# First part routed head by head, first tile's group norm in halves, output projection begun from the heads, one hold of the gathers taken out

## The chip, the core and the metric

The kernel runs on one core of one Trainium2 chip. The metric is the device time in microseconds (us) of one execution; less is better. The engines that matter here are TensorE (PE; its weight loads are PEld), VectorE (DVE), ScalarE (ACT), GpSimd (POOL), which issues the expert gathers, and SyncE (SP), which issues the weight and input transfers. Each engine works through its own instructions in the order written, and semaphores tie the engines together.

## What is computed

One layer of a decoder for a prompt of 512 tokens and a sample group of 8 x 4 tokens, model width 1024, all in float32. Cut to what matters here:

```python
p = rmsnorm(x) @ w_in                      # q, k, v, o for 4 heads; gates; a and g for the convolution
h = mlstm_chunkwise(q, k, v, gates, state) * sigmoid(o)
u = a * sigmoid(g)
c = silu(group_norm(depthwise_conv(u, 31 taps)))   # 8 groups of 64 channels
x = x + concat([h, c]) @ w_out
xn = rmsnorm(x)
q = xn @ w_query                           # 8 heads, two halves of 128
s1, s2 = q_half1 @ keys1, q_half2 @ keys2
# per token and head: top 16 of s1, top 16 of s2, top 16 of their sums -> 16 expert numbers
act = gelu(einsum(xn, u_tab[experts]))     # 128 rows of 1024 floats per token
x = x + einsum(softmax(scores) * act, v_tab[experts])
y = rmsnorm(x)
```

Each token reads 128 rows of the u table and 128 of the v table, 4 KB each.

## The kernel before, in words

**Tiles and groups.** The tokens make five tiles: tiles 1 to 4 are 128 prompt tokens each, tile 0 is the 32 sample tokens. The mixer works in three groups, (1), (2 and 0), (3 and 4). The experts are worked in the order 1, 2, 0, 3, 4. A pick is one expert number per partition: 128 picks for a prompt tile, 32 for the sample tile (its tokens are spread over four quadrants), 544 in all. Pick n needs one u gather and one v gather, 128 rows or 0.524 MB each. 32 picks (two of the eight heads) are a part; there are 17 parts, and part 9 (picks 288 to 319) is the first of tile 3.

**Gathers.** POOL issues them in the order of PLAN (`plan_gathers`, line 67): the u gathers run LEAD = 44 picks ahead of the v gathers, then u and v alternate. At a pick in LATE_PICKS, which are the first picks of tile 2 (128) and tile 3 (288), no u gather is issued before all v gathers below it. Every gather needs a free slot of 4 KB per partition: 12 slots at first, 14 from pick 160, 30 from pick 352 on (JOIN_AT), where weights and mixer buffers are no longer needed. A u gather also waits until its part's expert numbers exist (`picked`), a v gather for their transposed copy. A u slot comes free when VectorE has done its dot product (`dot_product`, line 1039), a v slot when TensorE has added a group of four (`experts`, line 859) into the PSUM tile y. The y tile is shared, so a tile's first group waits for the `final` of the tile before.

**Routing.** VectorE finds a part's expert numbers: `top_lists` (the best 16 of four score columns, two per head), `candidates` (sums of pairs and their best 16) and `experts_of` (a search by comparison over 16 x 50, per head). Between these steps it can take dot products (`between`).

**Order.** The mixer's steps are written out by hand for each engine; after each step an engine calls `keep`, which takes gather work up to a number that a list sets for that step: DOTS_BY (dot products on VectorE), QUADS_BY (groups of four v's on TensorE), GATES_BY (ACT). ROUTE_AT and ROUTE_DOTS say after which step and at which dot a part is routed, GATE_AT when its z columns are made, FINAL_AT when a tile's last norm is done. Two PSUM banks take all products of the mixer in turn (`order_of_banks`); a job needs the job two before it evacuated.

**First tile.** TensorE projects w_in in 24 weight tiles of 0.5 MB from a ring of four slots; SP requests the next one when the job that used the slot is done. VectorE does the 31 taps of the convolution for the channel chunks 0, 1 and then 2, 3 (`convolutions`). After it the four chunks are centred, squared, averaged, rooted, scaled and passed through silu together (`by_group`, `centre`, `squares`, `deviations`, `scale`, `silus`; NORMS names which chunks go together). Only then the output projection runs, eight jobs of 128 columns (`output`, `residual`), then transposes, queries and scores. `routing(1, 0)` starts when the four score columns of two heads are there; the first gather waits for it.

## Time and profile before

| | us |
|---|---|
| median of 3 runs | 1776.27 |
| range | 1767.8 to 1779.16 |
| profiled execution | 1774.04 |
| its span | 1772.2 |
| busy: PE / DVE / ACT / POOL | 1064.4 / 1065.0 / 333.7 / 1056.1 |

The profile is of one execution; its span goes from the first to the last instruction. Busy time is the sum over the span of one engine's instructions; the engines overlap. Of the expert work, VectorE has 462 dot products into slots of the ring (430 of them with the prompt's x, 1218 ns each), TensorE the v products (L884). The chain of waits that ended last splits the span into PE 27%, DMA 25%, DVE 20%, POOL 16%, issue 7%, ACT 3%. In the page's strip of forty slices the transfer rate is 206, 164 and 266 GB/s in the first three and about 409 in most of those after the middle; the lowest later ones are 309, 336, 321 and 264.

### The profile page before, as it was taken

The numbers are of one execution on the slowest core, as the hardware profiler recorded it, in microseconds if no ns is written. First come the engines' busy times: TensorE is split into PE (matmuls) and PEld (weight loads), VectorE is DVE, ScalarE is ACT, GpSimd is POOL, SyncE is SP. The second block draws the span as 40 slices with busy tenths as digits, with TensorE's granted clock in tenths as the row PEclk, the third lists the DMA queues.
The fourth block names the chain that finished last, engine by engine and source line by source line (L and its number), as shares of the span: only waits on it lengthen the run. The fifth ranks groups of instructions, "written<-read, shape, count | busy, mean of one in ns | idle before, by whom it ended". The sixth has DMA issues, their size and how long they took to land.

```text
span 1772.2 us, 18241 instructions
## 1 busy us (share of the span) xinstructions
PE 1064.4 (60%) x6249; PEld 657.5 (37%) x6249; DVE 1065.0 (60%) x2715; ACT 333.7 (19%) x874; POOL 1056.1 (60%) x1131
## 2 busy tenths in 40 slices
PE   7898457978796938887894477023333433333344
PEld 6787446756674726666662011000000000000000
DVE  5547796665693198575464703995757585845420
ACT  3232113653141213540221000000000000000000
POOL 2005356666453576675556755747777777777771
PEclk9899789979898978998997588555555666566668
DMA  6589999999998999998999999969999999999997
GB/s 206 164 266 397 359 399 391 353 351 410 412 367 309 403 406 409 408 409 336 409 410 409 362 347 321 410 264 409 409 410 409 410 409 411 409 409 410 409 409 290
DMA packets 192850, 659.75 MB, mean 372 GB/s; under 512 B 32336, under 2 KB 32344, under 8 KB 192632
## 3 DMA queue, kind: packets, MB, share of 16 engines
q0 software_dynamic: 156672, 570.49, 82.1%
q1 hardware_dynamic: 35512, 86.01, 13.7%
q10 hardware_dynamic: 576, 2.10, 0.3%
q8 instruction: 51, 0.84, 0.2%
q14 instruction: 39, 0.32, 0.0%
HBM read 652.96 MB, written 5.16 MB: 371 GB/s over the span
## 4 chain that ended last, share of the span: by engine, by line
PE 27%; DMA 25%; DVE 20%; POOL 16%; issue 7%; ACT 3%; SPq 2%; ACTq 0%; POOLq 0%; DVEq 0%
DMA ring<-in_u_experts,expert_idx 14%; DVE ring L1053 10%; POOL ring L594 9%; PE y L884 9%; DMA ring<-in_v_experts,expert_idx_by_token 9%; PE pp L635 8%; PE pp L645 4%; PE pp L711 3%; POOL C_sample L594 2%; SPq L483 2%; DMA act_T<-in_v_experts,expert_idx_by_token 1%; POOL w_ring L594 1%; DVE hit L1410 1%; DVE lists L1412 1%; DVE hit L1408 1%
## 5 line engine op out<-in xcount | busy, mean ns | idle before, releaser
L1053 DVE SCALAR_TENSOR_TENSOR ring<-ring,x_normed 128x1024 f32<-128x1024 f32 x430 | 514.4, 1218 | 335.2 <-DMA ring<-in_u_experts,expert_idx 332.7
L594 POOL DMA_INDIRECT ring<-in_u_experts,expert_idx x462 | 446.1, 966 | 409.6 <-DVE expert_idx L1417 118.7
L884 PE MATMUL y<-ring,z_columns 128*32 128x512 f32 x1364 | 398.9, 761 | 228.5 <-DMA ring<-in_v_experts,expert_idx_by_token 114.0
L594 POOL DMA_INDIRECT ring<-in_v_experts,expert_idx_by_token x313 | 302.3, 966 | 161.1 <-issue 76.6
L635 PE MATMUL pp<-act_T,w_ring 128*128 128x128 f32 (+2 forms) x1728 | 299.1, 333 | 87.5 <-DVE scratch L1232 31.9
L635 PEld LDWEIGHTS pp<-act_T,w_ring 128*128 128x128 f32 x1728 | 266.3, 200 | 127.1 <-issue 88.7
L884 PE MATMUL y<-C_sample,z_columns 128*32 128x512 f32 x316 | 199.8, 907 | 85.2 <-DMA ring<-in_v_experts,expert_idx_by_token 72.0
L884 PE MATMUL y<-w_ring,z_columns 128*32 128x512 f32 x180 | 139.3, 1002 | 182.5 <-DMA ring<-in_v_experts,expert_idx_by_token 161.7
L884 PEld LDWEIGHTS y<-ring,z_columns 128*32 128x32 f32 x1364 | 77.7, 127 | 374.6 <-issue 299.3
L645 PE MATMUL pp<-w_ring,act_T 128*128 128x128 f32 (+1 forms) x960 | 122.1, 289 | 39.8 <-DVE scratch L1247 14.1
L645 PEld LDWEIGHTS pp<-w_ring,act_T 128*128 128x128 f32 (+1 forms) x960 | 115.6, 187 | 53.8 <-issue 38.8
L884 PEld LDWEIGHTS y<-w_ring,z_columns 128*32 128x32 f32 x180 | 21.5, 153 | 270.6 <-issue 270.6
L711 PE MATMUL pp<-u_prompt,tap_diag 128*128 128x128 f32 (+1 forms) x496 | 91.5, 344 | 3.6 <-ACT tap_diag L1671 3.6
L1775 ACT ACTIVATE score_minus_max<-score_minus_max 128x16 f32<-128x16 f32 x34 | 7.0, 206 | 456.3 <-DVE ring L1053 425.3
L1671 ACT ACTIVATE tap_diag<-ident,w_dw 128x128 f32<-128x128 f32 x248 | 84.7, 394 | 34.9 <-PE pp L711 32.3
L711 PEld LDWEIGHTS pp<-u_prompt,tap_diag 128*128 128x128 f32 x496 | 80.6, 197 | 20.7 <-issue 13.4
L594 POOL DMA_INDIRECT C_sample<-in_v_experts,expert_idx_by_token x75 | 73.4, 978 | 24.0 <-issue 21.3
L884 PE MATMUL y<-act_T,z_columns 128*32 128x512 f32 x80 | 68.9, 1014 | 23.0 <-DMA ring<-in_v_experts,expert_idx_by_token 19.8
L884 PEld LDWEIGHTS y<-C_sample,z_columns 128*32 128x32 f32 x316 | 32.7, 142 | 128.9 <-issue 128.9
L884 PE MATMUL y<-keys_T,z_columns 128*32 128x512 f32 x68 | 57.7, 999 | 13.2 <-DMA ring<-in_v_experts,expert_idx_by_token 13.2
L1053 DVE SCALAR_TENSOR_TENSOR ring<-ring,x_sample_normed 128x1024 f32<-128x1024 f32 x32 | 38.8, 1227 | 29.4 <-DMA ring<-in_u_experts,expert_idx 29.2
L1034 DVE RECIPROCAL rstd<-sum_squares 128x1 f32<-128x1 f32 (+1 forms) x5 | 0.8, 159 | 89.6 <-ACT sum_squares L1785 89.6
(299 smaller groups left out, 1528.7 us busy)
## 6 DMA issues: line engine op xcount, KB each, us to landing
w_ring<-in_w_all SPq DMA_DIRECT2D x144, 512.0 KB, 6.8
ring<-in_u_experts,expert_idx POOLq DMA_INDIRECT x462, 11.0
ring<-in_v_experts,expert_idx_by_token POOLq DMA_INDIRECT x313, 10.4
x_res<-in_x_prompt SPq DMA_DIRECT2D x4, 512.0 KB, 5.0
C_sample<-in_state_C SPq DMA_DIRECT2D x4, 512.0 KB, 12.0
out_C_s<-C_sample ACTq DMA_DIRECT2D x4, 512.0 KB, 11.8
out_y_p<-x_res SPq DMA_DIRECT2D x16, 128.0 KB
C_sample<-in_v_experts,expert_idx_by_token POOLq DMA_INDIRECT x75, 12.5
```

The lines of the kernel that those rows point to most:

```text
L483: sp.dma_start(o["n_s"], nsm[:, :, :]).then_inc(out_s, 16)
L594: pool.indirect_dma_start(out=slot[s], out_offset=None, in_=a["u_experts"] if kind == "u" else a["v_experts"], in_offset=bass.IndirectOffs ...
L635: ins = pe.matmul(p[:, 0:width], w[:, k, :], actT[:, k, 0:width], start=(k == 0), stop=(k == KC - 1))
L645: ins = pe.matmul(p[0:ROWS[t], i * 128:(i + 1) * 128], actT[:, k, cols_of(t)], w[:, k, :], start=(k == 0), stop=(k == KC - 1))
L711: ins = pe.matmul(p[:, 0:n], tap_diag[:, k % TAP_SLOTS, :], up[:, c, j:j + n], start=(j == 0), stop=(j == TAPS - 1))
L884: ins = pe.matmul(Y[low:low + 32, half * 512:(half + 1) * 512], zcols[:, part % 2, lo:lo + 32], rhs, start=False, stop=True, skip_group_ch ...
L1053: dve.scalar_tensor_tensor(out=slot[s], in0=slot[s], scalar=1.0, in1=xn_now[:, :] if t else xs[:, :], op0=ALU.mult, op1=ALU.mult, accum_ou ...
L1408: step(dve.tensor_tensor(hit, bc(iota[:, :], 1, shape), bc(posf[:, h, :], 2, shape), ALU.is_equal))
L1410: step(dve.tensor_tensor(hit, hit, bc(ceid[:, h, :], 1, shape), ALU.mult))
L1412: step(dve.tensor_reduce(eid[:, h, :], hit, AX.X, ALU.add))
L1671: A(tap_diag[:, k % TAP_SLOTS, :], ident[:, :], ACT.Copy, scale=wdw[:, c, j:j + 1]).then_inc(tap_made, 1)
L1775: step(A(s, s, ACT.Exp, accum_out=zsum[:, 2 * p + h:2 * p + h + 1]))
```

## The change

- **Hold.** LATE_PICKS keeps only the first pick of tile 2.
- **Routing.** Part 0 is routed head by head; the expert numbers of head 0 are written and announced by themselves, so `picked` counts one more. POOL waits for 1 before pick 0, for 2 before pick 16, and for one more than before at each later part. No dot products are taken within part 0's routing.
- **Group norm of tile 1.** NORMS["first"] has two steps, chunks 0, 1 and chunks 2, 3. The first half's mean, centring, square, variance, root, scaling and silu are placed among the projections and the taps of the second convolution run; the second half follows where the whole was.
- **Output projection of tile 1.** Two jobs of 512 columns (`output_first`). The first adds the four k steps of the heads for its four weight tiles before it waits for the silus. A new semaphore w_taken tells SP when each of the first three of four weight tiles has been read. The residual is added in two steps of 512, and each half is transposed when it is there.
- **Order of the front.** Gate columns and rows after four projections instead of before; the gate rows' steps on VectorE inside the taps; the Exp of the scores before the last two sigmoids.
- **Tables.** One Sqrt on a scratch column at the start of ACT, and one before its last norm.
- **Lists.** DOTS_BY, QUADS_BY, GATES_BY, ROUTE_AT, ROUTE_DOTS, GATE_AT, FINAL_AT and NORM_AT are new. VectorE has four steps fewer. At the same step DOTS_BY asks for 4 to 6 dots fewer in most of the second group and for 19 to 20 fewer in the third: its value at the third group's first step is 135 instead of 154, and the last one before the end 216 instead of 236; QUADS_BY ends at 49 groups instead of 54. Part 9 is routed at dot 258 (before 244), part 10 at 290 (276), part 9's z columns are made at 321 (340).

`top_lists`, `candidates` and `experts_of` take the heads as an argument and are otherwise the same.

```diff
 
-LATE_PICKS = [FIRST[g[0]] for g in GROUPS[1:]]
+LATE_PICKS = [FIRST[GROUPS[1][0]]]
...
-NORMS = {"first": (0, slice(0, 128), [(0, ALL)]), "second": (1, slice(0, 128), [(1, ALL)]),
-         "sample": (1, slice(128, 128 + NS), [(2, ALL)]), "rest": (2, slice(0, 256), [(3, slice(0, 2)), (4, slice(2, 4))])}
+NORMS = {"first": (0, slice(0, 128), [(0, slice(0, 2)), (1, slice(2, 4))]), "second": (1, slice(0, 128), [(2, ALL)]),
+         "sample": (1, slice(128, 128 + NS), [(3, ALL)]), "rest": (2, slice(0, 256), [(4, slice(0, 2)), (5, slice(2, 4))])}
...
-ROUTE_AT = [1000000, 81, 83, 86, 127, 127, 127, 128, 135, 158, 158, 158, 158, 158, 158, 158, 158]
-FINAL_AT = [[131, 128], [158, 288], [158, 290], [158, 461]]
+ROUTE_AT = [1000000, 77, 82, 85, 123, 123, 123, 124, 125, 154, 154, 154, 154, 154, 154, 154, 154]
+FINAL_AT = [[127, 135], [154, 302], [154, 333], [154, 461]]
...
-
-                        sp.wait_ge(pp_full, J[weight_job(n - W_SLOTS)] + 1)
+                        before = n - W_SLOTS - N_IN
+                        if 0 <= before < N_OUT and before % 4 < 3:
+                            sp.wait_ge(w_taken, before // 4 * 3 + before % 4 + 1)
+                        else:
+                            sp.wait_ge(pp_full, J[weight_job(n - W_SLOTS)] + 1)
                     sp.dma_start(W[:, n % W_SLOTS, :, :], a["w_all"][n % N_W]).then_inc(w_land[n % W_SLOTS], 16)
...
                     parts += 1
-                    pool.wait_ge(picked, parts)
+                    pool.wait_ge(picked, parts + 1 if n else 1)
+                if (kind, n) == ("u", TOPK):
+                    pool.wait_ge(picked, 2)
                 if kind == "v" and n % PART == 0 and t:
                     parts_v += 1
                     pool.wait_ge(picked_v, parts_v)
...
                         evacuated(pe, ("xT", t, half))
+                if g:
+                    gate_columns(g)
+
...
 
+            def output_first(i):
+
+                if i == 0:
+                    pe.wait_ge(att_done, 1)
+                p = job(("out", 0, i))
+                w = [weights(N_IN + 4 * i + j) for j in range(4)]
+                for ks in (range(0, 4), range(4, 8)) if i == 0 else (range(0, 8),):
+                    if i == 0 and ks[0]:
+                        keep()
+                        pe.wait_ge(mix_c, CC)
+                    for j in range(4):
+                        for k in ks:
+                            ins = pe.matmul(p[:, j * 128:(j + 1) * 128], actT[:, k, 0:128], w[j][:, k, :],
+                                            start=(j == 0 and k == 0), stop=(k == KC - 1), skip_group_check=True)
+                        if ks[-1] == KC - 1 and j < 3:
+                            ins.then_inc(w_taken, 1)
+                ins.then_inc(pp_full, 1)
+                keep()
...
                     if t == 0:
                         pe.wait_ge(diag_ready, DIAG_ORDER.index("residual") + 1)
                     for half in range(2):
+                        if g == 0:
+                            evacuated(pe, ("out", 0, half))
                         blocks = [slice((4 * half + i) * 128, (4 * half + i + 1) * 128) for i in range(4)]
                         if t:
                             transposes(("x2T", t, half), 128, lambda i: x[:, t, blocks[i]], 4, 1.0)
...
             inputs(0)
+            project_in(0, 0, 4)
+            gate_columns(0)
             pe.wait_ge(consts, N_CONST)
             p = job(("gffn",))
             pe.wait_ge(ld_gffn, 16)
             pe.transpose(p[:, 0:KC], gffn_rows, ident[0:KC, 0:KC]).then_inc(pp_full, 1)
-            project_in(0, 0, 16)
+            project_in(0, 4, 15)
+            by_group("mean", "first", 0)
+            project_in(0, 15, 16)
             scores_in_chunk(1)
             project_in(0, 16, 18)
             keys_by_rows(1)
-            project_in(0, 18, 24)
+            project_in(0, 18, 20)
+            by_group("var", "first", 0)
+            project_in(0, 20, 24)
             within_chunk(1)
-            by_group("mean", "first", 0)
-            by_group("var", "first", 0)
+            by_group("mean", "first", 1)
+            by_group("var", "first", 1)
             heads_back(1)
-            for j in range(N_OUT):
-                output(0, j)
+            output_first(0)
+            output_first(1)
             turned(0)
             for head in range(PH):
                 query_head(0, head)
...
                 if g == 0:
-                    ins = dve.tensor_tensor(x[:, 1, span], x[:, 1, span], p[:, 0:128], ALU.add)
+                    span = slice(j * 512, (j + 1) * 512)
+                    ins = dve.tensor_tensor(x[:, 1, span], x[:, 1, span], p[:, :], ALU.add)
                 elif g == 1:
...
                     between()
                 p = parts_before(t) + part
-                now = slice(PART * (p % 8), PART * (p % 8 + 1))
-                dve.tensor_copy(idx[:, now], eid.rearrange("p h k -> p (h k)")).then_inc(picked, 1)
-                dve.wait_ge(picked, p + 1)
+                at = PART * (p % 8)
+                now = slice(at + TOPK * heads[0], at + TOPK * (heads[-1] + 1))
+                dve.tensor_copy(idx[:, now], eid[:, heads[0]:heads[-1] + 1, :].rearrange("p h k -> p (h k)")).then_inc(picked, 1)
+                if heads[-1] == 0:
+                    return
+
+                dve.wait_ge(picked, p + 2)
+                now = slice(at, at + PART)
                 if t:
...
                 stretch[0] += 1
-                while done[0] < ROUTE_DOTS[p][stretch[0]]:
+                while p and done[0] < ROUTE_DOTS[p][stretch[0]]:
...
 
-                top_lists(t, part)
-                candidates(t, part)
-                experts_of(t, part)
+                for heads in ((0,), (1,)) if (t, part) == (1, 0) else ((0, 1),):
+                    top_lists(t, part, heads)
+                    candidates(t, part, heads)
+                    experts_of(t, part, heads)
...
             dve.wait_ge(consts, N_CONST)
-            gate_rows(0)
-            rows_after(0)
...
-            convolutions({12: lambda: exponents(1), 18: heads_of_first})
-            centre("first")
+            convolutions([{3: lambda: gate_rows(0), 16: lambda: rows_after(0)},
+                          {8: lambda: centre("first", 0), 12: lambda: exponents(1), 18: heads_of_first,
+                           24: lambda: scale("first", 0)}])
+            centre("first", 1)
             evacuated(dve, ("gffn",))
             normalise(1)
-            scale("first")
             new_state(1)
-            for j in range(N_OUT):
-                residual(0, j)
+            scale("first", 1)
+            residual(0, 0)
+            residual(0, 1)
             dve.wait_ge(x_sums, 1)
-            for j in (N_OUT - 2, N_OUT - 1):
+            for j in range(2):
                 evacuated(dve, ("out", 0, j))
...
 
+            act.wait_ge(consts, 1)
+            step(A(scratch[:, 0:1], eps[:, :], ACT.Sqrt))
             act.wait_ge(consts, C_IDENT)
             act.wait_ge(x_sums, 1)
             norm1(1)
             act.wait_ge(ld_gmix, 16)
             inputs(0)
+            project_in(0, 0, 4)
+            gate_rows(0)
             filled(act, ("gffn",))
             A(gffn[:, :], bank(("gffn",))[:, 0:KC], ACT.Copy).then_inc(free(("gffn",)), 1)
             log_rows(0)
-            project_in(0, 0, 4)
+            project_in(0, 4, 12)
             exp_rows(1)
-            project_in(0, 4, 20)
+            project_in(0, 12, 16)
+            squares("first", 0)
+            project_in(0, 16, 18)
             exp_scores(1)
+            project_in(0, 18, 20)
+            deviations("first", 0)
             project_in(0, 20, 24)
-            squares("first")
-            deviations("first")
-            silus("first")
+            silus("first", 0)
+            squares("first", 1)
+            deviations("first", 1)
+            silus("first", 1)
             for half in range(2):
                 spread_T("x2T", 1, half, gffn)
             act.wait_ge(x_sums, 2)
                 query_head(2, head)
             keep()
+            step(A(den[:, 0:1], eps[:, :], ACT.Sqrt))
             final(ORDER[-1])
```

## Rows read from the trace of the kernel before

**Rows 1.** Totals of the DMA engines, from part 2 of the page

```profile
DMA packets 192850, 659.75 MB, mean 372 GB/s; under 512 B 32336, under 2 KB 32344, under 8 KB 192632
```

**Rows 2.** Busy us by stretch: PE, PEld, DVE, ACT, POOL, clock, DMA share, GB/s

```profile
0.00:130.09 130.09, 105.72 (x840) 102.09 (x841) 67.40 (x236) 39.65 (x96) 9.98 (x44) 0.95 0.68 212
130.09:1037.00 906.91, 676.37 (x4252) 496.78 (x4250) 584.37 (x1501) 260.82 (x711) 543.35 (x557) 0.86 0.99 385
205.00:225.00 20.00, 13.36 (x83) 13.10 (x84) 8.44 (x23) 3.50 (x12) 2.60 (x3) 0.70 0.78 297
...
1037.00:1185.00 148.00, 65.46 (x165) 16.24 (x164) 90.94 (x246) 5.99 (x11) 84.11 (x89) 0.71 0.87 322
1185.00:1750.00 565.00, 209.64 (x948) 40.67 (x948) 320.86 (x730) 24.52 (x52) 418.65 (x443) 0.61 1.03 409
1750.00:1772.20 22.20, 7.16 (x52) 1.67 (x48) 1.45 (x2) 2.69 (x4) 0.00 (x0) 0.80 0.46 171
```

**Rows 3.** Timeline, way to the first gather: start, us, operation, [idle before it]

```profile
102.86 5.44 PE L635 MATMUL pp<-act_T,w_ring 128*128 128x128 f32 x32 [1.87 <-ACT act_T L1582]
...
109.25 0.37 ACT L1762 ACTIVATE region<-pp,rstd 128x128 f32<-128x128 f32 x1 [0.27 <-PE pp L854]
...
114.36 0.88 DVE L1353 MAX8 lists<-region 128x8 f32<-128x128 f32 x4 [9.79 <-ACT region L1762]
...
123.47 0.99 DVE L1408 TENSOR_TENSOR hit<-iota,lists 128x800 f32<-128x800 f32 x1
...
129.62 0.18 DVE L1417 CAST expert_idx<-lists 128x32 uint32<-128x32 f32 x1
...
130.09 1.11 POOL L594 DMA_INDIRECT ring<-in_u_experts,expert_idx  x1 [118.70 <-DVE expert_idx L1417]
...
136.47 1.85 POOL L594 DMA_INDIRECT ring<-in_u_experts,expert_idx  x1 [0.30 <-issue]
```

**Rows 4.** Timeline of the first tile's mixer, 0 to 84 us

```profile
5.76 1.28 ACT L1562 ACT_TABLE_LOAD   x1 [5.76 <-DVE act_T L1080]
...
25.96 0.43 DVE L1115 TENSOR_TENSOR u_prompt<-u_prompt,region 128x256 f32<-128x256 f32 x1 [3.35 <-ACT u_prompt L1623]
...
71.73 1.06 PE L699 MATMUL pp<-region,halves 128*128 128x128 f32 x8
...
76.27 3.35 DVE L1165 RECIPROCAL region<-region 128x512 f32<-128x512 f32 x1 [0.67 <-ACT region L1693]
...
80.38 1.65 ACT L1701 ACTIVATE act_T<-region,gn_bias,gn_gain 128x128 f32<-128x128 f32 x4 [2.85 <-DVE region L1167]
...
82.08 13.43 PE L645 MATMUL pp<-w_ring,act_T 128*128 128x128 f32 x96 [5.77 <-ACT act_T L1701]
```

**Rows 5.** Timeline around the routing of the fourth tile's first part

```profile
907.42 0.18 DVE L1417 CAST expert_idx<-lists 128x32 uint32<-128x32 f32 x1
...
994.01 1.75 POOL L594 DMA_INDIRECT ring<-in_v_experts,expert_idx_by_token  x1 [0.30 <-issue]
...
1002.67 1.76 POOL L594 DMA_INDIRECT ring<-in_u_experts,expert_idx  x1 [0.30 <-issue]
```

**Rows 6.** TensorE, groups by line and form, 1037 to 1094 us: count, busy, mean ns

```profile
L884 PE MATMUL y<-ring,z_columns 128*32 128x512 f32 x112 | 49.8, 596 | 0.0
```

**Rows 7.** Waits from 1037 to 1094 us: total, times, longest

```profile
POOL ring L594 <- PE y L884: 21.9, 8, 6.4
```

**Rows 8.** Waits from 1156 to 1176 us

```profile
POOL ring L594 <- PE y L884: 16.5, 1, 16.5
```

**Rows 9.** DMA issues, part 6 of the page: count, median us to landing

```profile
ring<-in_v_experts,expert_idx_by_token POOLq DMA_INDIRECT x313, 10.4
```

**Rows 10.** Timeline of TensorE around 647 us

```profile
647.16 5.31 PE L635 MATMUL pp<-act_T,w_ring 128*128 128x256 f32 x16 [21.15 <-DVE scratch L1232]
```

**Rows 11.** Timeline of POOL around 224 us

```profile
224.28 0.94 POOL L594 DMA_INDIRECT ring<-in_u_experts,expert_idx  x1 [15.66 <-DVE ring L1053]
```

**Rows 12.** Timeline of ACT at the end of the span

```profile
1765.19 1.28 ACT L1785 ACT_TABLE_LOAD   x1
```

132 lines of the change are left out of this document (83 added, 49 removed), and 42 rows, old and new, of tables (DOTS_BY, GATES_BY, QUADS_BY, ROUTE_DOTS).

## The prediction

> **What bounds the kernel now.** I read the transfer totals first, then a table of stretches, then the two places where the table shows a hole, then the instructions around them. The kernel moves 659.75 MB [rows 1]. Between 1185 and 1750 us it moves 409 GB/s without a break [rows 2]; the reader should see that no stretch of the table is faster, so 409 GB/s is this kernel's ceiling. At that rate 659.75 MB take 1613 us. The span is 1772.2 us, so about 160 us are transfer time not used. Each stretch's share is its length times (1 - rate/409) [rows 2]: 62.7 us before the first expert gather (130.09 us at 212 GB/s), 53.2 us from there to 1037 us (906.91 us at 385), 31.5 us from 1037 to 1185 us (148 us at 322), 12.9 us at the end (22.2 us at 171). A change that leaves the bytes alone is worth what it takes out of these four numbers. No engine's busy share says this: PE, DVE and POOL each stand at 60%.
>
> The sum is made against the profiled execution: 1774.04 us, which is its span plus 1.84 us. The three timed runs have a median of 1776.27, 0.13% above it, and the range 1767.8 to 1779.16.
>
> **Part 1, the way to the first gather.** POOL waited 118.70 us for the first expert numbers and issued its first gather at 130.09 [rows 3]. Working back, step by step:
>
> The first square root is issued with its table load on the path (5.76 to 7.06 us, 1.28 of it the load [rows 4]); the new Sqrt on a scratch column fetches that table while x is still arriving: 1.3 us gained. The gate rows with their Exp and Ln and the two loads leave their place in ACT's queue ahead of the first sigmoid, so the convolution on VectorE, whose first operand came at 25.96 [rows 4], can begin near 20. But little of that reaches the end. VectorE now has about 2.5 us of row arithmetic and a half centring and scaling (about 2.4 us) inside its tap loop, and TensorE's own queue has the second group mean behind the values and the in-chunk products, which ran to 71.7 [rows 4]. The Exp of the scores ahead of two sigmoids shortens a wait in the same loop, which only matters if VectorE is last. I put the second mean at 70.5, 1.2 us earlier.
>
> From the mean on, each step is on the path and works on half the columns. From the first mean to the end of the silus it was 10.3 us; the reciprocal (3.35 us for four chunks) is the row to see, and with the silus (1.65) it halves to 2.5 us less [rows 4]. The centring, square, root and product, all of 512 columns too, give about 1.2 more by the same pace, and about 1.3 comes back, because the head transposes' product now stands before the second scaling on VectorE. The last silu ends near 78.4 instead of 82.0.
>
> Output: eight jobs from 82.08, six of them with 96 records in 13.43 us [rows 4], the last ended near 99.5 behind a weight transfer. In the new order 32 of 128 records (at most 13.43 / 3 = 4.5 us) run before the silus end. What follows would take 10 to 13 us, but the last four weights and the 1 MB of keys (3.1 MB, 7.7 us at 409 GB/s) can only be requested as slots are taken, from about 79 us. I take 92.5 for the end and 95 for the first query, against 102.86 [rows 3]: 8 us earlier, of which 3.6 came from the norm. On the synchronous queue the keys and the next weights stay in their order, so nothing is overtaken there.
>
> Routing: it began at 114.36 after four score columns; two of them were there at 109.62 [rows 3]. That is 4.7 us. It took 15.3 us to the expert numbers at 129.62 [rows 3]: 6.1 us of searches from 123.47, of which one head needs half, and 9.1 us of lists and candidates before them, of which it needs more than half since the small candidate steps are mostly fixed cost; I take 5.3. That is 8.4 us, 6.9 less. The first gather then goes out at 130.1 - 8 - 4.7 - 6.9 = 110.5.
>
> Not all 19.6 us are gained. By 130.09 the unused 62.7 us left 67.4 us of transfer done; at 110.5 about four query weights (0.524 MB, 1.28 us each at 409 GB/s) have not yet been moved. The hole becomes 110.5 - 62.3 = 48.2: **14.5 us gained**. Lower end: only the routing steps move (11.6 us), less 5.1 us of weights: 6.5. Upper end: the whole conv start of 5.9 us comes through as well: 20.
>
> Beside the routing of head 1 POOL now issues gathers. Rows show what that can cost: the issue at 130.09 took 1.11 us, but the one at 136.47 took 1.85 beside an operation of VectorE with two SBUF inputs (L1047), and another 1.75 beside a search [rows 3, 5]. Twelve slots can be filled in that time; if half were slow, 6 x 0.7 = 4 us, inside the lower end. In a sentence the rest can do without: the Trainium skill, SBUF — State Buffer, section "Who interferes with whom", infers that such a tensor_tensor takes only the shared read port and that descriptor writing needs the write port; by that rule this cost would be 0, and the rows speak against it.
>
> **Part 2, the hold at pick 288.** LATE_PICKS loses its second entry. Before, POOL issued u gather 287 at 1002.67 [rows 5], then v gathers alone until 287 of those were out. These include the sample tile's, whose records on TensorE took 49.8 / 112 = 0.445 us each [rows 6], 16 to a group of four gathers: 7.1 us, or 1.78 us per gather where the transfer needs 1.28; POOL waited 21.9 us for it [rows 7]. Then a burst of u gathers alone made VectorE last, the z columns of the next tile were late, and POOL waited 16.5 us for TensorE [rows 8]. Both are the 31.5 us. With u and v in alternation a group of four v's comes each 8 x 1.28 = 10.3 us, more than 7.1. Is the routing in time? Its expert numbers stood ready at 907.42 [rows 5], so even the old order had 95 us to spare. The new list routes it at 258 dots; u 288 is issued 30 pairs after, less what is in flight (at most 14 slots), so 16 x 2.56 = 41 us against the 29 us of such a routing with its dots in between (15.3 + 11 x 1.22, the page's mean for a dot product). The hold could have been dropped for nothing. One thing is new: the final norm of the sample tile stands at dot 333 on VectorE, with 14 slots instead of 30; its last v needs about 10.4 us to land [rows 9], 7.1 us on TensorE and 3 us on ACT, about 5 us later than dot 332. I charge 3 us: **28.5 us gained**; ends 20 and 31.5.
>
> **Part 3, precedence on VectorE.** The lists ask for 4 to 6 dots fewer at the same step in the second group and 19 to 20 fewer in the third. Rows show what it answers to: TensorE stood idle 21.15 us before 647.16, behind a product of VectorE's that queued after dots [rows 10]. But the transfers ran on through most of that; where POOL starved was the other way round, 15.66 us before 224.28, when VectorE stood in mixer steps [rows 11]; that stretch lost 5.5 us [rows 2]. Work done sooner with the transfers full is worth nothing now and keeps the routing early. Cost or gain unknown; nearest row 5.5 us each way. I take 0, with -8 and +16.
>
> **Part 4, the tail.** A second early Sqrt takes the table load of 1.28 us before the last root [rows 12] off the path: 1.3 us gained, with nothing beside it that could take it back.
>
> Sum: 1772.2 - 14.5 - 28.5 - 1.3 = 1727.9, plus 1.84 = **1730 us**, 2.6% below the median.
>
> One more sentence that nothing hangs on: the Trainium skill, DMA: Bandwidth & Descriptors, section on where 436 GB/s comes from, lets HBM-to-SBUF traffic be bound at about 358 GB/s per core; then 659.75 MB would need 1843 us and no order could help, which the 409 GB/s of the trace contradicts.
>
> **Rivals.** (a) Both gains, nothing new: 1730, chance 0.60. (b) The front gives its lower end (6.5) and precedence opens two or three more holes of 5.5 us: 1772.2 - 6.5 - 28.5 - 1.3 + 14 + 1.8 = 1752; for it speaks that 14 slots (14 x 1.28) are only 18 us of cover while VectorE waits in a mixer step. Chance 0.24. (c) The mixer run earlier also closes a few holes of 5.5 us and the front gives 20: about 1710; chance 0.09. (d) The slower side: u 288 waits at the head of POOL's queue for expert numbers, and every v behind it waits too. Where the old order let v's through, each us of lateness is now a lost one. It costs more than the 43 us only when the third group's scores come over 80 us (41 - 29 of slack, plus 43, plus 18 to leave 1%) after dot 258; against it, those numbers were ready at 907. Result 1795; chance 0.04. (e) The gather stream doesn't change where it matters, since VectorE, which has the dots and the routings of four parts to do at once, gives the earlier start back, and the second hold is replaced by one at 333: about 1765; chance 0.03.
>
> A measurement of this kernel can tell 1% (about 18 us) from no change. Faster by more than that: (a), (c) and most of (b), 0.86; within: 0.09; slower: 0.05. The range takes (a) with its ends and most of (b) and (c): 1712 to 1757.
>
> **What would show it.** First gather near 110 and about 48 us unused before it; 409 GB/s through the place where u 288 follows u 287 by a v gather; the sample tile's records idle between groups. If the first hole shrinks by under 6 us, part 1 is wrong; if a drain with TensorE back to back appears again, part 2; if the sum of holes between them grows over 65 us, part 3. All of it fails if another stretch runs above 409 or the bytes change.

## Result and the profile after

The changed kernel takes 1752.69 us (median of 4 runs, 1748.21 to 1757.02) against 1777.72 us before (4 runs): a ratio of 0.9868, with a 95% interval of 0.982 to 0.9916, or 25 us. Measured again on another chip, beside other kernels, it took 1747.16 against 1776.57 us: 0.9846 (0.9822 to 0.9871), 29 us. The forecast was 46 us. The time lies in the range, at its upper side. All medians here are of fast executions: one execution of the kernel with weights and keys moved (below) took 1838.7 us at a granted clock of 0.65 instead of 0.78 and is left out of its median.

The same table of stretches as in [rows 2], for the kernel after, cut at its first gather, at 935 us, where it is in the sample tile's dot products, and at the end of the holes:

```profile
0.00:125.68 125.68, 96.42 (x742) 92.93 (x743) 62.21 (x206) 39.21 (x85) 9.93 (x44) 0.93 0.64 195
125.68:935.00 809.32, 667.03 (x4185) 509.15 (x4183) 533.60 (x1378) 262.14 (x719) 465.67 (x485) 0.89 1.01 389
935.00:1150.00 215.00, 110.52 (x312) 23.87 (x312) 138.69 (x339) 11.98 (x22) 157.37 (x153) 0.70 0.98 375
1150.00:1730.00 580.00, 212.52 (x964) 41.20 (x964) 337.76 (x802) 26.01 (x54) 427.45 (x452) 0.59 1.03 409
1730.00:1749.20 19.20, 7.36 (x48) 1.68 (x48) 1.45 (x2) 1.41 (x3) 0.00 (x0) 0.81 0.34 121
```

The ceiling is still 409 GB/s. By length times (1 - rate/409) the unused time is 65.8 us before the first gather (before 62.7), 39.6 us from there to 935, 17.9 us from 935 to 1150, and 13.5 us at the end (before 12.9): 136.8 us against 160.3. So the first hole, in which 14.5 us were forecast, is 3 us larger, although the first gather leaves 4.4 us earlier. The hold's region is where the time came from. The tail's gain does not show in this number, whose last cut is only a round figure, but it does in the rows: from the last copy on ScalarE to the first output transfer it is 2.99 us (1742.37 to 1745.36), where it was 4.27 us before (1764.06 to 1768.33), since no table load stands there now:

```profile
1742.37 1.02 ACT L1861 ACTIVATE x_res<-y 128x1024 f32<-128x1024 f32 x1 [56.17 <-PE y L925]
1743.52 0.29 ACT L1863 ACTIVATE sum_squares<-sum_squares,eps 128x1 f32<-128x1 f32 x1
```

The timeline of the kernel after between the output projection and the first gather, which answers to [rows 3]:

```profile
80.07 8.86 PE L835 MATMUL pp<-w_ring,act_T 128*128 128x128 f32 x64 [0.94 <-DVEq L1366]
98.38 9.88 PE L835 MATMUL pp<-w_ring,act_T 128*128 128x128 f32 x64 [9.45 <-DMA w_ring<-in_w_all]
108.30 0.69 DVE L1384 TENSOR_TENSOR x_res<-x_res,pp 128x512 f32<-128x512 f32 x1 [18.64 <-PE pp L835]
111.04 3.81 PE L650 MATMUL pp<-act_T,w_ring 128*128 128x128 f32 x32 [1.28 <-ACT act_T L1650]
115.81 0.37 ACT L1840 ACTIVATE region<-pp,rstd 128x128 f32<-128x128 f32 x1 [0.27 <-PE pp L895]
116.27 0.49 DVE L1405 MAX8 lists<-region 128x8 f32<-128x128 f32 x2 [3.52 <-ACT region L1840]
121.29 0.21 DVE L1450 MAX8 lists<-lists 128x8 f32<-128x50 f32 x1
123.16 0.99 DVE L1472 TENSOR_TENSOR hit<-hit,lists 128x800 f32<-128x800 f32 x1
125.21 0.17 DVE L1480 CAST expert_idx<-lists 128x16 uint32<-128x16 f32 x1
125.68 1.11 POOL L609 DMA_INDIRECT ring<-in_u_experts,expert_idx  x1 [114.34 <-DVE expert_idx L1480]
```

The routing behaves as forecast. It starts when two scores are there (116.27, right behind the evacuation at 115.81) and needs 8.9 us to the expert numbers at 125.21 (forecast 8.4). What is late is its input. The first query starts at 111.04, forecast 95, before 102.86. The second output job, 64 records, ends only at 108.3, and ahead of it TensorE stood idle for 9.45 us, released by a weight.

The queue that requests the weights, SyncE's, in the same stretch (start, us it was busy issuing or waiting, what it loads, how many):

```profile
86.29 1.22 SPq L457 DMA_DIRECT2D w_ring<-in_w_all  x2
87.55 0.43 SPq L473 DMA_DIRECT2D keys_T<-in_keys_T  x1
88.07 20.55 SPq L457 DMA_DIRECT2D w_ring<-in_w_all  x6
```

The first of the last weights is requested at 86.29, behind the last silus (they end at 83.24), since only the first job's second pass gives a slot back; from 76 to 86 us the profile shows no byte moved. The keys (1 MB) are requested at 87.55 and the next weights behind them. The entry of 20.55 us from 88.07 holds six weights and the waits between them: each can be requested only when a slot of the weight ring is free. The last weight of the output projection waits by the code for the end of the first output job (88.93), and the job that needs it asks for all four of its weights at its start. Transfers in one stretch of 18 us, first in the kernel before:

```profile
86.00:104.00 18.00, 15.55 (x130) 14.99 (x129) 3.43 (x10) 3.39 (x9) 0.00 (x0) 0.97 0.88 312
```

The same stretch of the kernel after:

```profile
86.00:104.00 18.00, 8.55 (x55) 8.39 (x54) 0.69 (x1) 0.00 (x0) 0.00 (x0) 0.72 0.54 183
```

And of the kernel after with the waits split and the keys requested earlier (an experiment below):

```profile
86.00:104.00 18.00, 14.87 (x124) 13.86 (x123) 3.04 (x7) 5.07 (x14) 0.00 (x0) 1.00 0.94 281
```

From 312 to 183 GB/s: 18 x 129 / 409 = 5.7 us of the front's gain are lost here alone, and TensorE is busy 8.55 us of the 18 instead of 15.55, at a granted clock of 0.72 instead of 0.97. The wait costs a second time: behind it the second output job takes 9.88 us at a granted clock of 0.73 (0.50, that is 1.2 GHz, until about 104 us, then 2.4 GHz), and without it, in the experiment, 7.78 us at 1.00.

The start of the timeline in the kernel before, a memset on POOL, the step on VectorE that scales the identity and the first transposes behind it:

```profile
7.14 1.79 POOL L548 MEMSET z_columns<- 128x2048 f32 x1
7.66 1.41 DVE L1088 TENSOR_SCALAR diag<-ident,rstd 128x128 f32<-128x128 f32 x1
9.12 3.14 PE L659 MATMUL pp<-diag,x_res 128*128 128x128 f32 x13 [9.12 <-DVE diag L1088]
```

The Sqrt on a scratch column moves the table load from 5.76 [rows 4] to 0.81, but that step is longer now. The same lines of the kernel after, with its second mean and the last silus:

```profile
0.81 1.28 ACT L1870 ACT_TABLE_LOAD   x1 [0.81 <-PEq L2020]
6.34 2.69 DVE L1134 TENSOR_SCALAR diag<-ident,rstd 128x128 f32<-128x128 f32 x1
7.09 1.79 POOL L561 MEMSET z_columns<- 128x2048 f32 x1
9.08 3.14 PE L674 MATMUL pp<-diag,x_res 128*128 128x128 f32 x13 [9.08 <-DVE diag L1134]
75.27 0.61 PE L718 MATMUL pp<-region,halves 128*128 128x128 f32 x4
82.36 0.88 ACT L1779 ACTIVATE act_T<-region,gn_bias,gn_gain 128x128 f32<-128x128 f32 x2 [2.42 <-DVE region L1217]
```

The same 128x128 multiplication took 2.69 us instead of 1.41, now that it starts at 6.34 instead of 7.66, and TensorE starts at 9.08 instead of 9.12. In both kernels it ends 0.14 or 0.15 us behind the end of POOL's memset of z_columns (8.93 before, 8.88 after). So it may have been held up by the memset; no run moved that. The second mean stands at 75.27 (forecast 70.5).

### The profile page after: what moved, and what is told of

Read it like the earlier page. It is cut to its first block, busy times and chain, and to the rows that moved or that the text cites. A ratio compares the mean times of both kernels' runs of the same rounds, so it can differ in the third digit from the quotient of the medians.

```text
span 1749.2 us, 18263 instructions
## 1 busy us (share of the span) xinstructions
PE 1093.8 (63%) x6249; PEld 668.8 (38%) x6249; DVE 1073.7 (61%) x2724; ACT 340.8 (19%) x883; POOL 1060.4 (61%) x1131
## 2 busy tenths in 40 slices
DMA packets 192850, 659.75 MB, mean 377 GB/s; under 512 B 32336, under 2 KB 32344, under 8 KB 192632
## 4 chain that ended last, share of the span: by engine, by line
DMA 29%; PE 24%; POOL 21%; DVE 12%; issue 9%; ACT 2%; SPq 2%; ACTq 0%; POOLq 0%; DVEq 0%
POOL ring L609 15%; DMA ring<-in_u_experts,expert_idx 12%; PE pp L650 9%; DMA ring<-in_v_experts,expert_idx_by_token 7%; PE y L925 6%; DVE ring L1100 5%; PE pp L660 3%; PE pp L730 2%; POOL C_sample L609 2%; SPq L496 2%; DMA act_T<-in_v_experts,expert_idx_by_token 1%; POOL w_ring L609 1%; DMA w_ring<-in_w_all 1%; DMA w_ring<-in_u_experts,expert_idx 1%; DMA act_T<-in_u_experts,expert_idx 1%
## 5 line engine op out<-in xcount | busy, mean ns | idle before, releaser
L1100 DVE SCALAR_TENSOR_TENSOR ring<-ring,x_normed 128x1024 f32<-128x1024 f32 x440 | 530.1, 1219 | 345.2 <-DMA ring<-in_u_experts,expert_idx 341.0
L609 POOL DMA_INDIRECT ring<-in_u_experts,expert_idx x472 | 452.7, 959 | 399.0 <-DVE expert_idx L1480 123.7
L925 PE MATMUL y<-ring,z_columns 128*32 128x512 f32 x1328 | 411.5, 794 | 232.4 <-DMA ring<-in_v_experts,expert_idx_by_token 169.8
L650 PE MATMUL pp<-act_T,w_ring 128*128 128x128 f32 (+2 forms) x1728 | 299.1, 332 | 43.5 <-DMA w_ring<-in_w_all 13.5
L925 PE MATMUL y<-C_sample,z_columns 128*32 128x512 f32 x352 | 233.0, 926 | 66.0 <-DMA ring<-in_v_experts,expert_idx_by_token 51.8
L660 PE MATMUL pp<-w_ring,act_T 128*128 128x128 f32 (+1 forms) x832 | 107.1, 291 | 27.8 <-DVE scratch L1297 10.8
L660 PEld LDWEIGHTS pp<-w_ring,act_T 128*128 128x128 f32 (+1 forms) x832 | 101.0, 186 | 41.5 <-issue 22.6
L609 POOL DMA_INDIRECT C_sample<-in_v_experts,expert_idx_by_token x80 | 77.7, 972 | 24.4 <-issue 24.1
L925 PEld LDWEIGHTS y<-C_sample,z_columns 128*32 128x32 f32 x352 | 38.4, 146 | 107.8 <-issue 107.8
L925 PE MATMUL y<-keys_T,z_columns 128*32 128x512 f32 x68 | 57.3, 994 | 13.2 <-DMA ring<-in_v_experts,expert_idx_by_token 13.2
L609 POOL DMA_INDIRECT w_ring<-in_v_experts,expert_idx_by_token x45 | 42.5, 944 | 13.7 <-issue 12.8
## 6 DMA issues: line engine op xcount, KB each, us to landing
out_C_s<-C_sample ACTq DMA_DIRECT2D x4, 512.0 KB, 11.5
```

What stands on the lines that cost most here:

```text
L609: pool.indirect_dma_start(out=slot[s], out_offset=None, in_=a["u_experts"] if kind == "u" else a["v_experts"], in_offset=bass.IndirectOffs ...
L650: ins = pe.matmul(p[:, 0:width], w[:, k, :], actT[:, k, 0:width], start=(k == 0), stop=(k == KC - 1))
L660: ins = pe.matmul(p[0:ROWS[t], i * 128:(i + 1) * 128], actT[:, k, cols_of(t)], w[:, k, :], start=(k == 0), stop=(k == KC - 1))
L925: ins = pe.matmul(Y[low:low + 32, half * 512:(half + 1) * 512], zcols[:, part % 2, lo:lo + 32], rhs, start=False, stop=True, skip_group_ch ...
L1100: dve.scalar_tensor_tensor(out=slot[s], in0=slot[s], scalar=1.0, in1=xn_now[:, :] if t else xs[:, :], op0=ALU.mult, op1=ALU.mult, accum_ou ...
```

## Experiments

Eleven kernels in four sets, five of them run a second time. Two of the chips (sets one and three) run everything some 11% slower: the kernel before takes 1975 and 1964 us there. The profiles there show 365 to 374 GB/s from 1300 to 1850 us, where the others have 409, and VectorE, ScalarE and POOL released again and again by "another core or an unknown queue" (148 to 206 us in sum on VectorE, 97 to 112 on POOL, none of it on the others). What moved the data slower there is not known. Ratios of those sets are told, but no sum is made with them. In the other two sets the kernel before takes 1776.6 and 1776.3 us, as in the first measurement.

All traces of the faster chips move the same 659.75 MB, which take 1613.1 us at 409 GB/s. So what is unused behind the first gather is the span less 1613.1 us, less what is unused before it:

| trace | first gather | GB/s before it | unused before it | unused behind it | span |
|---|---|---|---|---|---|
| before | 130.09 | 212 | 62.7 | 96.4 | 1772.2 |
| hold alone | 127.78 | 215 | 60.6 | 66.7 | 1740.4 |
| after | 125.68 | 195 | 65.8 | 70.3 | 1749.2 |
| after, second measurement | 121.56 | 205 | 60.6 | 70.4 | 1744.1 |
| after, old lists | 123.33 | 198 | 63.6 | 62.2 | 1738.9 |
| after, sample rows in PSUM | 125.29 | 196 | 65.2 | 62.5 | 1740.8 |
| after, weights and keys moved | 113.14 | 217 | 53.1 | 66.7 | 1732.9 |
| best1 | 112.78 | 218 | 52.7 | 61.5 | 1727.3 |
| best1, routed whole | 124.75 | 217 | 58.6 | 67.4 | 1739.1 |

Each row is one execution, and the times of one kernel in one set spread over 3 to 13 us (17 in one case), so a difference of 3 us between two rows says little by itself.

**The hold alone.** The kernel before, with one entry of the list of late picks gone and the counts that depend on it (also the routing counts from part 10 on, and one entry each of GATE_AT and NORM_AT):

```diff
-LATE_PICKS = [FIRST[g[0]] for g in GROUPS[1:]]
+LATE_PICKS = [FIRST[GROUPS[1][0]]]
...
-FINAL_AT = [[131, 128], [158, 288], [158, 290], [158, 461]]
+FINAL_AT = [[131, 128], [158, 302], [158, 333], [158, 461]]
```

> The kernel before with the hold at pick 288 alone taken away: the list of late picks keeps one entry, the sample tile's final step moves to dot products 302 and 333, and three entries of the routing counts move with it; front, precedence and tail stay as before. Theory (part 2 of the prediction, re-sized by the trace of after): 19 us of the change come from here, so the span falls to 1749 to 1756 and the ratio is about 0.989; between 1000 and 1190 us about 18 us stay unused, because POOL's issues beside the sample tile's dot products take 1.8 us. Rival, as forecast: 28 us, ratio 0.984, 9 us unused, and the rest of the change then costs time.

> The kernel before with the hold alone taken away, a second time, since the chip of the first time was 11% slower. Theory: on a chip where before takes 1777 us this gives 19 us (ratio 0.989). Rival, as forecast: 28 us, ratio 0.984.

Measured: 0.9808 (0.9774 to 0.9843) on the slower chip; 1744.56 us, 0.9832 (0.9803 to 0.9861), on the other: 32 us. The rival is right and my re-sizing from the trace of after was wrong: the whole of the 28.5 us is there, and the one edit is worth as much as the full change (0.9832 and 0.9846 beside each other, with intervals that overlap). The stretch that moves the bytes between 350 and 450 MB, in the kernel before:

```profile
965.00:1247.00 282.00, 117.37 (x392) 26.15 (x392) 165.01 (x416) 14.00 (x28) 187.57 (x190) 0.63 0.93 356
```

Without the hold:

```profile
959.00:1213.00 254.00, 128.89 (x392) 27.11 (x384) 167.83 (x414) 15.28 (x29) 181.93 (x190) 0.63 1.00 394
```

In the kernel after, second measurement:

```profile
959.00:1217.00 258.00, 127.22 (x388) 26.90 (x380) 166.50 (x410) 15.28 (x29) 188.84 (x192) 0.67 1.00 388
```

And in the kernel after with the old lists:

```profile
958.00:1212.00 254.00, 129.09 (x392) 27.14 (x387) 166.58 (x412) 15.28 (x29) 181.98 (x190) 0.65 1.00 395
```

The unused time there is 36.5 us before, 9.3 without the hold, 13.2 in the kernel after, and 8.7 in the kernel after with the old lists (the next experiment but one): 27.2 us gained by the hold, 4.5 lost again by something else in the change.

**The hold put back** into the kernel after (the same lines reversed):

> The kernel after with the hold at pick 288 put back (list of late picks, final, norm and gate thresholds around it as before). Theory: 19 us more than after, ratio to before 0.996 to 1.000, profiled span about 1768. Rival (the hold is worth the forecast 28): 1777 or more, ratio over 1.002, that is the rest of the change costs 5 us.

Measured on the slower chip: 0.9992 (0.997 to 1.0014). Everything else in the change, taken together, is worth nothing that can be measured there. The ratio is the theory's, the reason is not: the hold alone is worth 1.9% on that chip, and by the next experiment, on another chip, the other parts give and take.

**The precedence lists.** The kernel after, unchanged, and with the six lists of the kernel before, shifted to its numbers, and the first entries of FINAL_AT and NORM_AT with them (the edit in outline):

```diff
-DOTS_BY, QUADS_BY, GATES_BY, ROUTE_AT, ROUTE_DOTS, GATE_AT = (after's)
+DOTS_BY = DOTS_BY_before[4:]; QUADS_BY = QUADS_BY_before[3:]; GATES_BY = [0, 0, 0] + GATES_BY_before; ...
```

> The kernel after, unchanged, beside the others of this set on the same chip, since the first set ran on a chip on which the kernel before took 1975 us instead of 1777. Expected: ratio to before 0.985 to 0.989 where before takes 1777 again; on a chip like the last one, 0.983 (the value between its relatives: single wait moved 0.981, hold put back 0.999).

> The kernel after with the lists of the kernel before, shifted to its job numbers (how many dot products, expert products and gate steps each engine may be ahead of a mixer step), so that the precedence of the mixer steps alone is undone; front, hold and tail stay as after. Theory: precedence gives about 7 us between 140 and 940 us (unused transfer time there 45 instead of 38 us), so this takes 5 to 9 us more than after. Rival 1 (forecast, precedence is worth nothing): within 2 us of after. Rival 2 (the new lists cost time, and the shorter front wait hides it): 3 us or more less than after.

Measured: after 1747.16 (0.9846), with old lists 1739.95 us (0.9798, 0.9774 to 0.9822). The second rival is right: the new lists cost 7.2 us by the medians, with intervals that only touch. In the traces 8.2 us less is unused behind the first gather (62.2 against 70.4), 4.5 of it in the stretch from 350 to 450 MB.

> The kernel after with the lists of before up to the 127th VectorE step, the 208th TensorE job and the 200th ScalarE step, and its own lists behind these. Its own lists allow 49 expert products instead of 54 and 216 dot products instead of 236 at the mixer's end. Theory (the backlog at the mixer's end costs the time): as after, 5 to 8 us above the kernel with all old lists (ratio 0.984). Rival (what costs is the middle, between 60 and 150 MB, where after left 18 us unused and the old lists 12): as the old lists, ratio 0.980.

Measured on a slower chip: 0.9861 (0.9829 to 0.9892), where best1 (below) has 0.9787. That is 0.74% more, but best1 also has the front's edits (7 to 8 us, 0.4%), and neither the kernel after nor the one with all old lists was run on this chip. It leans to the end of the mixer as the place where the new lists cost, and shows no more.

**What the end of the mixer does.** The gathers that POOL issues in the kernel after, second measurement, where the sample tile's dot products run (start, us, operation), and those dot products on VectorE:

```profile
933.39 1.87 POOL L609 DMA_INDIRECT ring<-in_u_experts,expert_idx  x1 [0.30 <-issue]
940.67 1.63 POOL L609 DMA_INDIRECT ring<-in_v_experts,expert_idx_by_token  x1 [0.31 <-issue]
942.60 1.98 POOL L609 DMA_INDIRECT ring<-in_u_experts,expert_idx  x1 [0.30 <-issue]
944.89 1.75 POOL L609 DMA_INDIRECT ring<-in_v_experts,expert_idx_by_token  x1 [0.30 <-issue]
948.19 1.76 POOL L609 DMA_INDIRECT C_sample<-in_v_experts,expert_idx_by_token  x1 [0.30 <-issue]
933.22 1.23 DVE L1100 SCALAR_TENSOR_TENSOR ring<-ring,x_sample_normed 128x1024 f32<-128x1024 f32 x1
942.54 1.22 DVE L1100 SCALAR_TENSOR_TENSOR ring<-ring,x_sample_normed 128x1024 f32<-128x1024 f32 x1
947.91 1.23 DVE L1100 SCALAR_TENSOR_TENSOR ring<-ring,x_sample_normed 128x1024 f32<-128x1024 f32 x1
```

The same with the old lists:

```profile
951.32 1.23 DVE L1074 SCALAR_TENSOR_TENSOR ring<-ring,x_sample_normed 128x1024 f32<-128x1024 f32 x1 [1.34 <-DMA ring<-in_u_experts,expert_idx]
951.52 1.83 POOL L583 DMA_INDIRECT ring<-in_u_experts,expert_idx  x1 [0.74 <-PE y L899]
953.87 1.22 DVE L1074 SCALAR_TENSOR_TENSOR ring<-ring,x_sample_normed 128x1024 f32<-128x1024 f32 x1 [1.31 <-DMA ring<-in_u_experts,expert_idx]
954.91 0.99 POOL L583 DMA_INDIRECT ring<-in_u_experts,expert_idx  x1 [0.30 <-issue]
```

Usually an issue takes 0.94 us, and with 0.30 us between issues that is just under the 1.28 us that a transfer of 0.524 MB needs. An issue of 1.6 to 2.0 us is more. The sample tile's dot products read both operands from SBUF, and the rows show when an issue beside them gets long. The issue at 942.60 begins inside the dot product of 942.54 to 943.76 and ends at 944.58, 0.82 us behind it; the one at 951.52 begins inside a dot product that ends at 952.55 and ends at 953.35, 0.80 behind it; the one at 954.91 begins just before a dot product ends (955.09) and ends at 955.90, 0.81 behind it. Of the 27 issues that begin inside a sample dot product between 850 and 1070 us in the kernel after, 26 end 0.80 to 0.82 us behind it (the other, begun 0.04 us after its start, took 0.93), and so do all 29 with the old lists. The dot products of the other tiles, which read one operand from PSUM, do nothing of the kind: 33 and 28 issues begin inside them, and all take 0.93 to 0.95 us. Two of the five long issues above (940.67 and 944.89) stand beside the searches of a routing, which also read two operands from SBUF.

So what counts is at which point of the dot product an issue begins. With the old lists 31 of the 32 sample dot products wait for their row, most of them 1.3 us, and the two engines keep step: one issue begins 0.2 us before a dot product and takes 0.94, the next 0.2 to 0.3 us before its end and takes 1.0. With the new lists 11 of the 32 run without a wait, and many issues begin early in one. Between 860 and 1060 us, 18 issues take over 1.3 us (13.5 us over 0.94 in sum), 14 of them beside sample dot products and 4 beside searches; in the first trace of the kernel after it is 16 (11.5 us), with the old lists 4 (2.9 us). That the step is lost because VectorE comes out of the mixer with a backlog is my reading; no run shows it by itself. So their rows were put in PSUM:

```diff
+                    dve.tensor_copy(xn_now[:, :], xs[:, :]).then_inc(xn_ready, 1)
-   in1=xn_now[:, :] if t else xs[:, :],
+   in1=xn_now[:, :],
```

> The kernel after with the sample tile's normed rows copied to PSUM once (one copy added), so that its 32 dot products read one operand from SBUF instead of two; nothing else changed. In after, 18 gather issues of POOL between 860 and 1060 us take over 1.3 us (13.5 us over the usual 0.94 in sum), with the old lists 4 (2.9 us). Theory (the new lists cost time because those dot products then run where POOL has a backlog): the slow issues go and the time falls by 5 to 9 us, ratio to before 0.980 where before takes 1777. Rival (the smaller lead of expert products costs it): slow issues go, time within 2 us of after, 0.984.

Measured: 1742.60 us, 0.9799 (0.9775 to 0.9822), 4.6 us less than the kernel after (on another chip, where before takes the same), or 0.5% by the ratios, whose intervals only touch. Slow issues 5 (3.2 us) instead of 18, all five beside searches or other operations with 128x1024 operands, none beside a sample dot product. The unused time behind the first gather is 62.5 us, as with the old lists (62.2), against 70.4. The rival is put aside: most of what the lists cost is this. The stretch from 350 to 450 MB agrees, 252 us at 397 GB/s, 7.4 us unused against 13.2:

```profile
963.00:1215.00 252.00, 124.48 (x392) 26.43 (x384) 167.42 (x412) 15.28 (x29) 183.34 (x191) 0.72 1.01 397
952.35 1.50 POOL L609 DMA_INDIRECT ring<-in_u_experts,expert_idx  x1 [0.30 <-DVE ring L1103]
1006.38 1.64 POOL L609 DMA_INDIRECT ring<-in_v_experts,expert_idx_by_token  x1 [0.31 <-issue]
```

**The weights of the output projection.** Each waited for where it is used, and the keys requested earlier:

```diff
-                w = [weights(N_IN + 4 * i + j) for j in range(4)]
                     for j in range(4):
+                        w = weights(N_IN + 4 * i + j)
...
-            load_w(20, 30)
+            load_w(20, 28)
             sp.dma_start(keys_flat[:, :], ...)
-            load_w(30, 36)
+            load_w(28, 36)
```

> The kernel after with the first tile's output projection waiting for each 128-column weight where it is used instead of for all four at its start. Theory: the wait for the last weight stays, but only behind 48 of the 64 matmuls: 6 to 7 of the 9.45 us of idle time before the second output job go, the first gather is at 118 to 120 instead of 125.7, and the time is 4 to 6 us less than after's (ratio to before 0.983 to 0.985). Rival 1 (the request of the last weight, not the wait, sets it and a whole transfer has to follow): first gather within 2 us of 125.7. Rival 2 (the front's gain is given back in the middle): first gather earlier, time the same as after's.

> The kernel after with both: each output weight waited for where it is used, and the 1 MB of keys requested before the last two weights that fit the ring instead of behind them. Theory: the second output job starts without a wait, first gather at 115 to 118, unused transfer time before it 8 us less, time 7 to 9 us less than after's (ratio to before about 0.982). Rival 1: keys ahead delay the weights of the projections, and the first gather is no earlier than with the single wait moved. Rival 2: first gather earlier, time as after's, since VectorE has the same work to do behind it and the buffers come free no sooner.

> Each output weight waited for where it is used, and the keys requested before the last two weights, a second time beside after itself. Theory: first gather at 113 to 116, time 8 to 12 us less than after's on the same chip. Rival (given back later): first gather 10 us earlier, time within 3 us of after's.

Measured: the first alone 0.9811 (0.9781 to 0.9841), both 0.9761 (0.9728 to 0.9793) on the slower chip, with the first gather at 119.07 and 113.76; both together on the chip of the kernel after 1739.11 us, 0.9813 (0.9782 to 0.9845), 8.0 us less than it by the medians (5.9 by the ratios, whose intervals overlap), with the first gather at 113.14 instead of 121.56. On the slower chip the kernel with the hold put back has the front of the kernel after; its first gather is at 121.23. There the wait alone brings 2.2 us, where I had expected 6 to 8, and the earlier keys 5.3 us more. The timeline of TensorE with both edits, on the chip of the kernel after:

```profile
79.73 7.17 PE L835 MATMUL pp<-w_ring,act_T 128*128 128x128 f32 x57
87.96 7.78 PE L835 MATMUL pp<-w_ring,act_T 128*128 128x128 f32 x64 [1.06 <-DMA w_ring<-in_w_all]
95.57 0.60 PE L636 MATMUL pp<-ident,x_res 128*128 128x128 f32 x4
98.51 3.81 PE L650 MATMUL pp<-act_T,w_ring 128*128 128x128 f32 x32 [1.28 <-ACT act_T L1650]
```

The wait (8.22 us in the trace of the kernel after on this chip) is down to 1.06. The gather is 8.4 us earlier and 7.5 us less is unused before it (53.1 against 60.6): here nearly all of it arrives.

**Together**, with the old lists (best1), and best1 with the first part routed whole again, and with the sample rows in PSUM. The edit that undoes the split:

```diff
-for heads in ((0,), (1,)) if (t, part) == (1, 0) else ((0, 1),):
+for heads in ((0, 1),):
...
```

> The kernel after with three edits that the sets before point to: each output weight waited for where it is used, keys requested before the last two weights, and the ahead-of lists of the kernel before (precedence undone). On a chip where before takes 1777: if the 7.7 us of the first two and the 7.2 us of the lists add up, 1732 us (ratio 0.975); if both empty the same unused time, 1738 (ratio 0.978). First gather at 113 to 115 either way.

> best1 (each output weight waited for where used, keys earlier, old lists) a second time, since the set before ran on a chip on which before takes 1964 us. Where before takes 1777: 1732 (0.975) if the gains of the front and of the lists add up, 1738 (0.978) if not.

> best1 with the first part of the first tile routed whole (both heads together) again, as in the kernel before. Theory: the first gather comes 6 to 7 us later and is preceded by four scores instead of two (4.7 us more): 123 to 126, but the weights of the next group move meanwhile, so that the time rises by only 3 to 6 us over best1. Rival: the full 11 us come back in the time.

> best1 with the first part routed whole, a second time. On the slower chip it cost the same time as best1 (0.980 and 0.979), with the first gather 8 us later. Theory as forecast: 3 to 6 us more than best1. Rival: nothing, because while the first gather is late the weights of the next group use the transfers.

> best1 with the sample tile's normed rows copied to PSUM once, so that its 32 dot products read one operand from SBUF instead of two (one copy of 1.2 us added). Theory: the 10 to 16 gather issues of POOL that take 1.75 to 1.99 us beside these dot products instead of 0.94 fall to 0.94 to 1.1, and the time by 3 to 8 us. Rival: the issues get short, but the transfers queue anyway (a backlog of 10 us stands behind them): time within 2 us of best1.

> best1 with the sample tile's rows in PSUM, a second time. In best1 only 3 to 4 issues are slow (2.6 us in sum), so 0 to 3 us are to be had: 1729 to 1732 where best1 takes 1732. Rival: the copy and its waits cost more than that.

| kernel | slower chip, ratio | other chip, us | ratio, interval | first gather |
|---|---|---|---|---|
| best1 | 0.9787 | 1734.66 | 0.9757 (0.9733 to 0.9782) | 112.78 |
| best1, routed whole | 0.9799 | 1739.99 | 0.9789 (0.9762 to 0.9816) | 124.75 |
| best1, rows in PSUM | 0.9781 | 1730.66 | 0.9735 (0.9712 to 0.9757) | 115.23 |

The gains of the front and of the lists mostly add: 1734.7, between the two numbers that I had given. The split of the routing is worth 5.3 us of time by the medians, with intervals that overlap, for 12 us in the first gather; 5.9 us more is unused before that gather without it. The rows in PSUM give 4 us more in the median, with intervals that overlap. That last kernel is the best found: 46 us, or 2.6%, under the kernel before, 1% under the changed one. On the slower chip the three can't be told apart, and the old lists show no gain there (0.9787, against 0.9761 without them on the other slower chip).

## Why the prediction was wrong

The terms, from medians of one set, on a chip where before takes 1776.57 us:

| step | forecast | measured | from |
|---|---|---|---|
| hold | 28.5 | 32.0 | before - hold alone |
| front and tail | 14.5 + 1.3 | 4.6 | hold alone - after with old lists |
| precedence | 0 (-8 to +16) | -7.2 | after with old lists - after |
| sum | 44.3 | 29.4 | before - after |

The ratios of two neighbours in this table differ by 0.3 to 0.5% with intervals of 0.2 to 0.3% to each side, so the 4.6 us are not clear of nothing, and the 7.2 us only just. The hold's 32.0 us are clear.

**Part 2 was right.** The size is the forecast's, a little over; in the traces 29.7 us less is unused behind the first gather (66.7 against 96.4). Of its reasons, the two drains [rows 6 to 8] went: POOL waited 42.5 us for TensorE's v products between 935 and 1190 us before, and 12.6 us between 935 and 1150 after. The sample tile's final step at dot 333 costs what was charged for it. TensorE waits 5.9 us for it, and POOL 6.27 us for a slot behind that:

```profile
POOL ring L609 <- PE y L925: 12.6, 5, 6.3
PE y L911 <- DVE x_res L1083: 10.2, 2, 5.9
1064.19 0.94 POOL L609 DMA_INDIRECT ring<-in_u_experts,expert_idx  x1 [6.27 <-PE y L925]
```

From 1060 to 1070 us the transfers run at 292 and 247 GB/s (5 us each), so 3.4 us are unused there; the forecast had charged 3.

**Part 1 is the step that failed**, at one sentence: "I take 92.5 for the end and 95 for the first query". The output ended at 108.3 and the first query came at 111.04. I had seen that "the last four weights and the 1 MB of keys can only be requested as slots are taken", and then let them cost transfer time (7.7 us) from 79 us. The silus ended at 83.24 instead of 78.4, the first request came at 86.29 instead of 79, and the last weight was there at 98.38, 12.1 us later: the job's four weights were one wait, the fourth was behind the keys and behind the end of the first job, and so transfers stood in line after 64 records instead of beside them. The output then ended 15.8 us later than I took. With the two edits it ended at 95.7 and the first gather came at 113.1, 2.6 us from the forecast, and the time fell by 8.0. By the prediction's own sign (first hole shrinks by under 6 us) part 1 is wrong: of its 14.5 us, the two traces of the kernel after show 3 us more and 2 us less unused before the first gather, and with the old lists it is 3 us more than with the hold alone. Smaller misses: the second mean came at 75.27 against 70.5 (73.42 in the second measurement, where the first 64 records of the projection took 7.38 us instead of 9.36); I read the rest from the new order, with gates and three table loads (26.43 to 30.95 us) between the chunks, and didn't test it. The Sqrt's 1.3 us was eaten by the longer multiplication behind it, though I had written that it would be gained. The routing steps were nearly right: 4.7 us as forecast for the start, and 8.9 us from first search to number, 6.4 less instead of 6.9; their undoing costs 12 us in the gather.

The step from gather to time also was too generous: 4.4 us earlier in the first profile left 3 us more unused, as 3.1 MB less had been moved by then (24.5 against 27.6 MB). The prediction took off 5.1 us for weights not yet moved at a gather 19.6 us earlier; here 7.5 us (3.1 MB) were missing at one only 4.4 us earlier.

**Part 3** was mis-sized within its bounds: "I take 0, with -8 and +16", measured -7.2 (a loss). The mechanism I named, POOL starving behind mixer steps of VectorE [rows 11], is not what the runs show; the loss came around the mixer's end, from gather issues that begin inside the sample tile's dot products and are held until those end. The rows for it were in the prediction, as a charge on the front: 1.85 and 1.75 us beside operations of VectorE with two SBUF inputs [rows 3, 5]. The prediction weighed an inference of the Trainium skill (SBUF — State Buffer, "Who interferes with whom"), by which that cost is 0, and took the rows; the runs bear the rows out: moving one operand to PSUM took the slow issues from 18 to 5. I did not ask which tiles' dot products have that form, nor where the new lists put them.

**Part 4** was right by the rows: 1.3 us forecast, and the path from the last copy to the first output transfer is 1.28 us shorter (2.99 against 4.27). In the run times so small a gain can't be seen, and it wasn't tried alone.

Of the rivals, (b) has the right signs: it gave the front's lower end and a loss by precedence, 1752 us; it had 0.24 where (a) had 0.60. That the first measurement hit its number to 1 us is in part luck: it charged 14 us to holes of POOL behind mixer steps, which are not what cost, and the measured loss is half of that, while the front gave less than its lower end. One sum in rival (d) is off too: 12 + 43 + 18 is 73 us, not over 80; nothing hangs on it, as no wait of that kind came. What stays open: how much of the lists' 7.2 us is slow issues (4.6 us by the medians of the PSUM run, 7.9 by its trace), where the 4.6 us of front and tail arise, if they are real, and whether the front with the projection order of before would reach the second mean earlier; the last wasn't tried.

## What to carry to other kernels

When a stage is shortened, list the requests behind it: a transfer that can be asked for only when a slot comes free is timed by the consumer, so a shorter consumer needs the request moved too, and a wait for several weights at the start of a job is a wait for the last one. Undo one part at a time before sizing it from two traces: from the trace of after I had put the hold at 19 us, since another part's loss lay in the same stretch, and the kernel with that edit alone gave 32. And where rows of the profile show an operation of one engine holding up another's, ask of the whole kernel which operations have that form, and what a new order puts beside them.

## What the runs showed of the hardware

An issue of a gather of 128 rows of 4 KB takes POOL 0.94 us, with 0.30 us to the next. An issue that begins while VectorE runs a scalar_tensor_tensor of 128x1024 with both operands in SBUF ends 0.80 to 0.82 us behind that operation, so it takes up to 2.0 us (26 of 27 in the kernel after, 29 of 29 with the old lists); one that begins before such an operation, or inside one with an operand in PSUM, takes 0.94 in nearly all. A multiplication of 128x128 by VectorE took 1.41 or 2.69 us with only its start moved by 1.3 us, and ended 0.15 us behind a memset of POOL both times; that the memset held it wasn't tested. The same program took 1776 to 1778 us in three measurements and 1964 and 1975 in two others, on other chips, where the steady stretch moves about 371 GB/s instead of 409; there the removal of the hold was worth the same 2%, and most edits behind it could not be told apart.
